# Column sums, key scores and gate tiles reordered, and late modulation tiles held back until the key tiles have landed

## Time and profile before

| | |
|---|---|
| median of 3 runs | 1880.55 us (1879.61 to 1883.78) |
| the profiled execution | 1882.81 us, its span 1880.9 us |
| PE busy | 1685.9 us (90% of the span) |
| DVE, ACT, POOL busy | 917.1, 556.4, 325.5 us |
| mean DMA rate, bytes | 299 GB/s, 563 MB |
| chain that ended last | PE 67%, DMA 18%, DVE 7%, ACT 4%, issue 3% |

### The profile page before, as it was taken

The page is one execution under the profiler, slowest core; times in us unless marked ns, Lnnn a source line. Parts: engine busy times, 40 slices in busy tenths (PEclk is TensorE's granted clock), DMA queues, the critical chain, the costliest instruction groups (busy, mean ns, idle before and its releaser), DMA issues.

```text
span 1880.9 us, 30536 instructions
## 1 busy us (share of the span) xinstructions
PE 1685.9 (90%) x12330; PEld 1587.4 (84%) x12330; DVE 917.1 (49%) x2286; ACT 556.4 (30%) x1511; POOL 325.5 (17%) x301
## 2 busy tenths in 40 slices
PE   4999999989999878878898899877699999999998
PEld 4788878878789777768898898866699999989998
DVE  5641375552255677666887855459633210231200
ACT  0111224740033444434565321225513110132100
POOL 0100000000022444434324321226300000020000
PEclk9998999999999999999999999988799999999999
DMA  8962348324359999999999999999867988755783
GB/s 360 378 237 98 116 128 251 135 90 157 137 207 411 415 421 420 421 419 421 411 418 410 421 420 421 421 380 390 331 232 251 326 294 296 254 185 202 271 292 132
DMA packets 85434, 563.15 MB, mean 299 GB/s; under 512 B 8832, under 2 KB 17568, under 8 KB 17968
## 3 DMA queue, kind: packets, MB, share of 16 engines
q0 software_dynamic: 39776, 289.46, 37.5%
q1 hardware_dynamic: 38992, 256.05, 36.4%
q10 hardware_dynamic: 6528, 15.72, 2.9%
HBM read 556.96 MB, written 4.23 MB: 298 GB/s over the span
## 4 chain that ended last, share of the span: by engine, by line
PE 67%; DMA 18%; DVE 7%; ACT 4%; issue 3%; POOL 0%; ACTq 0%; SPq 0%; DVEq 0%
PE PS L886 30%; PE PS L633 21%; DMA AUX<-in_peer_uv_dram,SCR 8%; PE PS L850 7%; DMA ring<-in_stream_dram 6%; DMA V<-in_peer_uv_dram,SCR 3%; DVE PROJ L2067 2%; DMA CONV<-in_peer_uv_dram,SCR 1%; PE PS L704 1%; PE PS L655 1%; PE PS L679 1%; PE PS L753 1%; ACT PROJ L1403 1%; ACT small L1395 0%; PE PS L1000 0%
## 5 line engine op out<-in xcount | busy, mean ns | idle before, releaser
L633 PE MATMUL PS<-H,ring 128*128 128x256 f32 x1280 | 290.1, 388 | 7.6 <-DMA ring<-in_stream_dram 4.0
L633 PEld LDWEIGHTS PS<-H,ring 128*128 128x128 f32 x1280 | 247.6, 195 | 44.0 <-issue 9.6
L850 PE MATMUL PS<-PROJ,AUX 128*128 128x128 f32 x1632 | 214.2, 293 | 73.1 <-ACT PROJ L1403 72.9
L850 PEld LDWEIGHTS PS<-PROJ,AUX 128*128 128x128 f32 x1632 | 204.5, 207 | 80.8 <-ACT PROJ L1403 80.6
L886 PE MATMUL PS<-H,ring 128*128 128x128 f32 x2272 | 261.9, 276 | 4.0 <-DMA ring<-in_stream_dram 2.3
L886 PEld LDWEIGHTS PS<-H,ring 128*128 128x128 f32 x2272 | 258.3, 193 | 5.2 <-issue 4.3
L1207 POOL DMA_INDIRECT AUX<-in_peer_uv_dram,SCR x124 | 143.1, 1154 | 476.9 <-DVE SCR L2051 215.9
L850 PE MATMUL PS<-PROJ,CONV 128*128 128x128 f32 x1328 | 168.0, 287 | 45.1 <-ACT PROJ L1403 45.1
L850 PEld LDWEIGHTS PS<-PROJ,CONV 128*128 128x128 f32 x1328 | 161.2, 202 | 50.2 <-ACT PROJ L1403 50.0
L886 PE MATMUL PS<-PROJ,ring 128*128 128x128 f32 x1664 | 192.6, 276 | 9.3 <-DMA ring<-in_stream_dram 9.3
L886 PEld LDWEIGHTS PS<-PROJ,ring 128*128 128x128 f32 x1664 | 188.9, 192 | 11.5 <-DMA ring<-in_stream_dram 9.5
(11 more groups left out here) (338 smaller groups left out, 1879.2 us busy)
## 6 DMA issues: line engine op xcount, KB each, us to landing
ring<-in_stream_dram SPq DMA_DIRECT2D x185, 1024.0 KB
AUX<-in_stream_dram SPq DMA_DIRECT2D x51, 1024.0 KB, 4.9
AUX<-in_ada_dram POOLq DMA_DIRECT2D x16, 1024.0 KB, 9.5
PROJ<-in_ada_dram ACTq DMA_DIRECT2D x4, 1024.0 KB, 20.3
AUX<-in_ada_dram SPq DMA_DIRECT2D x4, 1024.0 KB, 19.8
bias_skewed<-AUX ACTq DMA_DIRECT2D x1, 3072.0 KB, 41.9
ring<-in_stream_dram ACTq DMA_DIRECT2D x2, 1024.0 KB
PROJ<-in_rgw_dram ACTq DMA_DIRECT2D x2, 1024.0 KB, 10.4
```

Of the source, the lines that this page charges most:

```text
L633: mm = pe.matmul(acc(n, c), w[:, k, c * P:(c + 1) * P], src[:, g * DC + k, :], start=(g == 0 and k == 0 and (c == 0 or groups == 1)), stop ...
L850: mm = pe.matmul(y_chunk(t, c), UV[b][:, D + c * P:D + (c + 1) * P], DIAG[turn % ND], start=(k == 0 and c % 4 == 0), stop=(k == SPT - 1), ...
```

## The change

Six edits, as the diff shows. POOL waits for a second landing in each ring slot, that is for the four k tiles, before it issues the late w_ada tiles. The gate tiles g3 to g7 are projected ahead of pairs 2, 5, 8, 11 and 13 and copied out at heads 10, 16, 22 and 28 and behind the loop; ACT then waits for the last two to be out before the sigmoid. The first four of the eight products of `mean1` stand between out tiles 2 and 3. H behind the first layer norm is made by ACT from the normed X, and no longer by DVE; the fetch of the sub-keys and the scaling of X follow on ACT. The key scores of query tile 0 are taken right behind that tile, ahead of the transposes of H, and copied out there. The order of banks follows.

```diff
@@ plan_jobs
-    jobs += [("h2", i) for i in range(4)]
-    jobs += [("sc", c) for c in range(16)]
+    jobs += [("sc", 0), ("sc", 1)] + [("h2", i) for i in range(4)]
+    jobs += [("sc", c) for c in range(2, 16)]
+GATE_TILES = (2, 5, 8, 11, 13)
@@ PE, scan
-                if pair in (2, 4, 6, 8, 10):
-                    project("g", 2 + pair // 2, H)
+                if pair in GATE_TILES:
+                    project("g", 3 + GATE_TILES.index(pair), H)
@@ PE, out and mean1
-            for t in range(4):
+            for t in range(3):
                 project("out", t, MIX, ready=None if t else taken_from("ssd"))
-            sum_chunks("mean1", X, DC, ready=taken_from("out"))
+            o = open_bank(pe, "mean1")
+            add_chunks(o, range(0, 4))
+            project("out", 3, MIX)
+            made(add_chunks(o, range(4, 8)), "mean1")
@@ PE, queries
                 if t == 0:
+                    key_scores(0)
                     for i in range(4):
...
-                else:
+                elif t > 1:
                     key_scores(t - 1)
@@ POOL, ahead of the late w_ada tiles
-                pool.wait_ge(S(f"tile_landed{s}"), 16)
+                pool.wait_ge(S(f"tile_landed{s}"), 32)
@@ ACT, scan
-                if h % 4 == 2 and 6 <= h <= 26:
-                    g_out((h + 2) // 4)
+                if h == 6:
+                    g_out(2)
+                if h % 2 == 0 and h // 2 - 3 in GATE_TILES:
+                    g_out(3 + GATE_TILES.index(h // 2 - 3))
             decay(SSD_HEADS - 1)
+            g_out(7)
+            wait_evacuated(act, "g", 6)
+            wait_evacuated(act, "g", 7)
@@ ACT, behind norm_help(1)
+            for c in range(DC):
+                act.wait_ge(S("x_normed"), c + 1)
+                act.activation(H[:, c, :], X[:, c, :], ACT.Identity, scale=H_GAIN[:, c:c + 1], bias=H_SHIFT[:, c:c + 1])\
+                    .then_inc(S("h_ready"), 1)
             act.dma_start(PROJ[:, 70, :], io["sk"]).then_inc(S("sk_landed"), 16)
             for c in range(DC):
-                act.wait_ge(S("h_ready"), DC + c + 1)
                 act.activation(X[:, c, :], ...
@@ ACT, queries
                 if t == 0:
+                    score_out(0)
...
-                if t:
+                if t > 1:
                     score_out(t - 1)
@@ DVE, behind center(1)
             for c in range(DC):
                 dve.tensor_tensor(X[:, c, :], H[:, c, :], RS[:, :], ALU.mult).then_inc(S("x_normed"), 1)
-                if c:
-                    dve.wait_ge(S("x_normed"), c)
-                    dve.tensor_scalar(H[:, c - 1, :], X[:, c - 1, :], ...).then_inc(S("h_ready"), 1)
-            dve.wait_ge(S("x_normed"), DC)
-            dve.tensor_scalar(H[:, DC - 1, :], X[:, DC - 1, :], ...).then_inc(S("h_ready"), 1)
```

More of the change, by code:

```diff
@@ L825, in _, with add_chunks @@
                 project("ssd", t, YS, 2, ready=None if t else lambda k: pe.wait_ge(S("ys_ready"), k + 1))
-            for t in range(4):
+            def add_chunks(o, chunks):
+                ready = taken_from("out")
+                for k in chunks:
+                    ready(k)
+                    mm = pe.matmul(o[:, 0:TOK], ones, X[:, k, :], start=(k == 0), stop=(k == DC - 1), skip_group_check=True)
+                return mm
+            for t in range(3):
                 project("out", t, MIX, ready=None if t else taken_from("ssd"))
-            sum_chunks("mean1", X, DC, ready=taken_from("out"))
+            o = open_bank(pe, "mean1")
+            add_chunks(o, range(0, 4))
+            project("out", 3, MIX)
+            made(add_chunks(o, range(4, 8)), "mean1")
             sum_chunks("var1", PROJ[:, 48:56, :], DC, ready=lambda k: pe.wait_ge(S("ln_square"), k + 1))
@@ L1988, in _ @@
                 dve.tensor_tensor(X[:, c, :], H[:, c, :], RS[:, :], ALU.mult).then_inc(S("x_normed"), 1)
-                if c:
-                    dve.wait_ge(S("x_normed"), c)
-                    dve.tensor_scalar(H[:, c - 1, :], X[:, c - 1, :], H_GAIN[:, c - 1:c], H_SHIFT[:, c - 1:c], ALU.mult, ALU.add)\
-                        .then_inc(S("h_ready"), 1)
-            dve.wait_ge(S("x_normed"), DC)
-            dve.tensor_scalar(H[:, DC - 1, :], X[:, DC - 1, :], H_GAIN[:, DC - 1:DC], H_SHIFT[:, DC - 1:DC], ALU.mult, ALU.add)\
-                .then_inc(S("h_ready"), 1)
             def top16(rows_, vals, idx):
```

## The result

The changed kernel takes 1892.07 us (median of 6 runs, 1886.54 to 1896.86), the kernel before in the same job 1880.19 us (6 runs, 1874.80 to 1883.78). The ratio is 1.0069, with a 95% interval of 1.0054 to 1.0084. It is slower, as forecast, but by 11.9 us and not by 5.3, and the median lies 0.07 us above the top of the forecast's range. The profiled execution took 1892.64 us, its span is 1891.0.

What follows compares the result with a forecast made beforehand. The prediction took the kernel as bound by a chain 67% PE and 18% DMA. Its terms, +8.3 - 3.5 + 0 + 0.5 = +5.3 us, put the median at 1885.8 us (profiled execution 1888.1), range 1877 to 1892.

Steps and rivals of the forecast that it cites:

- A: Start through head 0: holding the late tiles back costs +8.3 us in all, from +1 to +14.
- A, the gain: Key tiles at the start: PE loses its 4.0 us wait and 3.1 us of half clock, gaining 7.1 us.
- A, DVE's lateness: Late tiles on DVE: last pair starts at 138.5, ends at 144.7, da_diff at 150.3; step +5.9 us (+1.1 to +10.8).
- A, what PE does meanwhile: Before head 0: three xbc tiles bring PE to the transposes at 137.3, where it waits 13 us for da_diff.
- A, the clock: Behind PE's long wait at head 0: the lowered clock costs +2.4 us (0 to +3.5).
- B: Scan: spread gate tiles start attn 1.8 us earlier and shorten it 1.7 us; -3.5 us, bounds -8.5 to +3.
- Rival 2: Scan: short idles halve the clock in each group; B +3, the whole +11.8, 1892.3 us; chance 0.10.
- Rival 3: Stall at its lower bound, scan gains more: A +4, B -7, D 0.5; -2.5, 1878.0 us; chance 0.15.
- C: Column sums: moving four products of mean1 ahead of the last out tile changes 0 us (-0.4 to +0.5).
- D: Queries: H on ACT and key scores of tile 0 first cost +0.5 us (0 to +2).
- Rival 4: Gather stage: the eight early gathers pay 8 us; the whole -2.7, 1877.8 us; chance 0.06.
- Rival 1: Head 0: DVE catches up, ending at 127.2; A -7.1, the whole -10.1, 1870.4 us; chance 0.07.

Runs made afterwards that it cites:

- experiment 3: The changed kernel with ACT copying head 0's three xbc tiles out before that head's exponentials: 1891.84 us, ratio 1.0075.
- experiment 10: The kernel of experiment 3 plus 52 overwritten 128x256 products on PE ahead of its wait for da_diff: 1893.87 us, ratio 1.0073.
- experiment 7: The kernel before with the query edits alone (H on ACT, key scores of tile 0 first): 1879.86 us, ratio 0.9998.
- experiment 4: The changed kernel with the first four late tiles not held, the rest held for the first key tile only: 1873.76 us, ratio 0.9974.
- experiment 11: The kernel before with the gate tiles spread and the first-key-tile hold ahead of the fifth late tile: 1872.96 us, ratio 0.9960.
- experiment 6: The kernel before with only the gate tiles and their copies moved: 1876.70 us, ratio 0.9985.
- experiment 9: The changed kernel again, unaltered, timed on the same chip as experiment 10: 1891.93 us, ratio 1.0072.
- experiment 5: Experiments 3 and 4 together, on the changed kernel: 1878.41 us, ratio 0.9999.
- experiment 12: The kernel of experiment 11 with the first-key-tile hold ahead of the seventh late tile instead of the fifth: 1874.93 us, ratio 0.9979.

## Why the prediction went wrong

**A, the gain.** Held. No wait for the first key tile, 27.87 us for the four (forecast 27.7), clock 1.00. The q tiles ended 1.2 us later than reckoned in this execution, so that the value tiles came 5.7 us earlier, not 7.1; nothing hangs on it, since PE waits afterwards. That the late tiles beside it delay the first key tile is shown by its wait, gone here. But the "5 us instead of 2.5" that the prediction worked out for this is smaller than the trace's 8.86 against 4.9: the direction agrees, the size does not.

**A, DVE's lateness.** Its end held, in part by luck. The last pair began at 138.50 (138.5 forecast), DVE ended at 144.65 (144.7) and `da_diff` at 150.2 (150.3). But two misses cancel in that. The last key tile landed at 69.5 (67.7), since its slot came free only when PE had used the last q tile, at 61.8, and the first pair began at 79.4 (78); the pairs then came every 8.44 us (8.65).

**A, what PE does meanwhile.** This step failed: "three xbc tiles at 6.91 us each bring PE to the transposes of head 0 at ... 137.3", and PE "waits 13 us for it". I took the xbc tiles for work that lies beside DVE's lateness, and asked only what is queued behind `da_scores(0)` on DVE. The question had to be asked of ACT too: `da_exp(0)` waits there for DVE, and behind it stand the copies that empty the two banks PE alternates between. So PE had two tiles of cover, not three; the third started at 148.87, 11.3 us later than the 137.5 of the kernel before, where the forecast had the stall at +5.9. Experiment 3 moved the copies and got what the forecast had drawn: an idle of 12.73 us (13) and the transposes at 150.41 (150.3). The Trainium skill asks that independent groups of products rotate through PSUM banks, so that the evacuation of one overlaps the next ("Perfetto Trace Analysis", section "Matmuls"); here two banks do rotate, and it did not help, because the evacuating engine was itself waiting.

**A, the clock.** Mis-sized. I took +2.4 us (0 to +3.5). The third xbc tile ran at 0.50 to 0.52 for its first 6 us and took 10.08 us instead of 6.91 (+3.0 at the transposes), and +1.7 went in the next three xbc tiles (22.65 instead of 20.97): 4.7 us. Had PE waited as forecast, the clock would have cost more, some 6 us by experiments 3 and 10. The prediction's reason for a low price, that the small products of head 0 lose less, did not hold: in experiment 3 they and the dt products alone lost 5.0 us. The sum of A was +8.3, with bounds of +1 and +14; measured +16.05 at the scan: 11.3 of wait, 4.7 of clock. Even with the other order on ACT the step would have been +6.0 of wait and +5.8 of clock, which is the +11.8 that experiment 3 shows at the transposes of x (335.28 against 323.50).

**B.** Held: -1.7 to the attn tiles and -1.4 in them, -3.1 against -3.5. Idles of 1.6 us ahead of pairs 4, 7 and 10, none ahead of 13 to 15, and the attn tiles at full speed. By itself 0.9985, -2.8 us by the ratio. Rival 2 (the half clock in each group) did not happen: the gate tiles took 7.17 us each, as before, and no row shows the 3.3 us of half clock per group of its bound. That the time came out near its 1892.3 is chance. Rival 3 (A at +4, B at -7) did not happen either.

**C.** Held: 0.

**D.** Held in sign: +1.0 at the first weighed value against +0.5, of which 0.79 is the wait ahead of the key scores (forecast 0.7). The gathers started 8.6 us earlier relative to PE, gather 8 did not, and experiment 7 finds no gain in time. Rival 4 is out with its 8 us; the 3.1 us by which the stage is shorter in the profiles with these edits stay open.

**The sum** at the first weighed value: +16.05 - 3.1 + 0 + 1.0 = +13.9, where the forecast had +5.3. Of the 8.6 us between them, A has 7.8. The medians say +11.9.

**Rival 1** decided at a DVE end of 131.7. In the change DVE ended at 144.65, and it waited for tiles ahead of every pair. In experiments 4 and 11, where it has two pairs behind it, it ended at 129.4 and 126.8, and PE's gain is there: the transposes at 140.62 and 138.25, and 0.26 and 0.40% in time, of which the gate tiles are 0.15% by experiment 6.

**Open.** In experiment 3, 3.3 us were left at the first weighed value (569.63 against 572.92; 2.2 against experiment 9) and its median is 0.1 to 0.2 us below that of the changed kernel. The intervals of the two ratios are each 0.15% (2.8 us) to either side, so the medians can't tell 2 or 3 us from none; I don't know whether they are there.

## What to carry to other kernels

When a result will come late, ask of every in-order queue that waits for it, not only of the last one, what stands behind the waiting instruction; above all whether an engine that empties PSUM banks is among them: here PE's cover then ended after two tiles, one for each bank. A transfer that feeds a long serial chain (here eight pairs of 6.15 us) should not be held back in favour of one that is late once by 4 us. Hold only what the chain doesn't need yet, and keep the first tiles. And time the parts of a change alone; here one part lost 16 us and another gained 3.

## What the runs showed of the hardware

Behind an idle of 12.73 us, PE was busy without a gap from 150.4 on, and the granted clock was still 0.50 in the window from 161 to 164 us; what it did in between were the transposes, head 0's small products and the dt products (128x32 each), and then 128x256 products again. Behind the longer idle of 16.82 us, with an xbc tile of 128x256 products first, the clock was 1.00 from 155 us on, 6 us after the idle (windows of the changed kernel):

```profile
150.00:155.00 5.00, 5.00 (x14) 3.93 (x13) 0.19 (x1) 0.00 (x0) 0.00 (x0) 0.52 0.00 0
155.00:158.00 3.00, 3.00 (x16) 2.64 (x15) 0.00 (x0) 0.00 (x0) 0.00 (x0) 1.00 0.00 0
...
164.00:167.00 3.00, 3.00 (x13) 2.50 (x13) 2.20 (x10) 0.00 (x0) 0.00 (x0) 0.67 0.03 5
167.00:170.00 3.00, 3.00 (x12) 2.55 (x11) 0.01 (x1) 0.00 (x0) 0.00 (x0) 0.76 0.00 0
```

There it fell again, to 0.67 and 0.76, after the dt products, with no idle of PE before it; before the change and in experiment 10 the same products left it at 1.00. In experiment 5, behind an idle of 4.49 us and with the same small products first, it was back at 0.99 from 146 to 149 us, and fell to 0.50 from 149 to 152, again behind the dt products. So small products do not always keep it at half, and what tells these cases apart no run here isolates; the price in the changed kernel is the +1.7 us above.

The half clock of the key tiles before the change stood, with the DMAs at a share of 1.01, just behind an idle of 4.0 us; in the changed kernel the DMAs were as busy while PE kept 1.00 (62 to 65 us: share 1.01, 415 GB/s). In experiment 12 a wait of 3.76 us brought the slow key tiles back (29.55 us). These runs point to the wait, not to the transfers, as what cost the clock. In experiment 5 a wait of 4.49 us left it at 0.53 while the DMAs were all but idle (142 to 144 us: share 0.01).
